# The rotary halves of the queries exchanged by on-chip transfers in place of TensorE products, in a decoder step on one core

## The reference

```python
def rope(x, pos):
    inv = ROPE_THETA ** (-jnp.arange(0, QK_ROPE_DIM, 2, dtype=jnp.float32) / QK_ROPE_DIM)
    ang = pos[:, None] * inv[None, :]
    ...
    cos, sin = jnp.cos(ang), jnp.sin(ang)
    x1, x2 = jnp.split(x.astype(jnp.float32), 2, axis=-1)
    return jnp.concatenate([x1 * cos - x2 * sin, x2 * cos + x1 * sin], axis=-1).astype(x.dtype)

def mla_query(hn, w_dq, q_norm, w_uq, w_uk, pos):
    B, L, _ = hn.shape
    cq = rmsnorm(hn @ w_dq, q_norm)
    q = (cq @ w_uq).reshape(B, L, N_HEADS, QK_NOPE_DIM + QK_ROPE_DIM)
    q_nope, q_rope = q[..., :QK_NOPE_DIM], q[..., QK_NOPE_DIM:]
    q_rope = rope(q_rope, pos)
    q_lat = jnp.einsum('blhd,chd->blhc', q_nope, w_uk)
    return q_lat, q_rope
```

## Time and profile before

| | us |
|---|---|
| median of 3 runs | 737.13 (736.79 to 737.34) |
| the profiled execution | 736.92 |
| its span in the trace | 735.2 |
| TensorE busy in the span | 725.5 |
| GpSimd, ScalarE, VectorE busy | 534.0, 408.1, 306.4 |

### The profile page before, as it was taken

One profiled execution on the slowest core, in us unless ns is written; L12 is line 12 of the kernel. 1 busy time (PEld: TensorE's weight loads), 2 busy tenths in 40 slices (PEclk: granted clock), 3 DMA queues, 4 the chain that ended last, 5 costly groups with the idle time before them and its releaser, 6 DMA issues.

```text
span 735.2 us, 16667 instructions
## 1 busy us (share of the span) xinstructions
PE 725.5 (99%) x6251; PEld 709.0 (96%) x6251; DVE 306.4 (42%) x771; ACT 408.1 (56%) x741; POOL 534.0 (73%) x252
## 2 busy tenths in 40 slices
PE   9999999999999999999999999999999999999995
PEld 9999999999999999999999888799999999999994
DVE  5446986233323222232488766752233323221002
ACT  7877555455444444555677566654554444445442
POOL 5995778869878888889867122159878878888991
PEclk9999999999999999999999999999999999999998
DMA  7864445556776755565565898326556555555641
GB/s 261 274 201 141 133 158 181 196 173 223 246 234 233 233 175 184 195 202 195 180 250 191 292 374 299 127 80 208 173 160 195 189 177 187 178 172 199 201 144 60
DMA packets 44554, 144.68 MB, mean 197 GB/s; under 512 B 5618, under 2 KB 5874, under 8 KB 44242
## 3 DMA queue, kind: packets, MB, share of 16 engines
q1 hardware_dynamic: 44210, 143.50, 58.3%
q0 software_dynamic: 144, 0.40, 0.1%
q10 hardware_dynamic: 144, 0.02, 0.0%
HBM read 142.42 MB, written 1.48 MB: 196 GB/s over the span
## 4 chain that ended last, share of the span: by engine, by line
PE 98%; DVE 1%; ACT 1%; issue 0%; DVEq 0%; POOL 0%; POOLq 0%
PE ps L1329 29%; PE ps L1330 29%; PE ps L1331 29%; PE ps L1730 1%; PE ps L1706 1%; PE ps L1391 1%; PE ps L1392 1%; PE ps L1399 1%; PE ps L1650 1%; PE ps L1459 1%; PE ps L1374 1%; PE ps L1368 0%; PE ps L1577 0%; PE ps L1710 0%; PE ps L1636 0%; PE ps L1355 0%
## 5 line engine op out<-in xcount | busy, mean ns | idle before, releaser
L408 POOL TENSOR_TENSOR wlo<-raw,whi 128x1024 fp32r<-128x1024 f32 x221 | 526.6, 2406 | 182.8 <-ACT whi L474 182.8
L1329 PE MATMUL ps<-xhi,whi 128*128 128x264 f32 x1000 | 286.9, 287 | 0.0
L1330 PE MATMUL ps<-xlo,whi 128*128 128x264 f32 x1000 | 283.3, 283 | 0.0
L1331 PE MATMUL ps<-xhi,wlo 128*128 128x264 f32 x1000 | 283.2, 283 | 0.0
L474 ACT ACTIVATE whi<-raw 128x1024 fp32r<-128x1024 f32 x221 | 232.7, 1054 | 50.1 <-PE ps L1331 48.4
L1330 PEld LDWEIGHTS ps<-xlo,whi 128*128 128x128 f32 x1000 | 188.5, 189 | 0.2
L1329 PEld LDWEIGHTS ps<-xhi,whi 128*128 128x128 f32 x1000 | 188.3, 188 | 0.3
L1331 PEld LDWEIGHTS ps<-xhi,wlo 128*128 128x128 f32 x1000 | 187.5, 188 | 0.0
L1329 PE MATMUL ps<-ahi,whi 128*128 128x264 f32 x352 | 100.0, 284 | 0.0
L1331 PE MATMUL ps<-ahi,wlo 128*128 128x264 f32 x352 | 99.9, 284 | 0.0
L1330 PE MATMUL ps<-alo,whi 128*128 128x264 f32 x352 | 99.9, 284 | 0.0
(11 more groups left out here) (259 smaller groups left out, 1146.5 us busy)
## 6 DMA issues: line engine op xcount, KB each, us to landing
raw<-w_stream SPq DMA_DIRECT2D x221, 512.0 KB, 3.3
pg<-pages SPq DMA_DIRECT2D x64, 288.0 KB, 4.3
pg<-w_ukT SPq DMA_DIRECT2D x1, 2048.0 KB, 9.4
pg<-w_uv SPq DMA_DIRECT2D x1, 2048.0 KB, 9.4
h<-xT SPq DMA_DIRECT2D x4, 264.0 KB, 4.5
y_out<-h SPq DMA_DIRECT2D x4, 264.0 KB, 2.7
raw<-w_stream SPq DMA_DIRECT2D x4, 256.0 KB, 5.0
wsraw<-wsT SPq DMA_DIRECT2D x1, 512.0 KB, 5.4
```

Source lines behind the costliest of these rows:

```text
L408: pool.tensor_tensor(wlo[:, c % RING, :], raw[:, c % RING, :], whi[:, c % RING, :].bitcast(F32), ALU.subtract).then_inc(lo_ready, 1)
L1329: pe.matmul(out, whi_, mhi, start=start, stop=False)
L1330: pe.matmul(out, whi_, mlo, start=False, stop=False)
L1331: return pe.matmul(out, wlo_, mhi, start=False, stop=stop)
```

## The change

Three things change.

1. The exchange is done by four transfers per pair, issued on SyncE: each moves one strip of 32 partitions x 264 numbers of the sines' product `tt` to the neighbouring strip of `sq`. TensorE's `query_swap` is gone. VectorE writes the cosines' product to the pair's PSUM bank itself, and the sum waits for all four transfers (`rope_swapped`).
2. With the swaps gone, TensorE, VectorE and ScalarE take the pairs one at a time. ScalarE writes a head's high part ahead of its sample columns, and copies the turned pair p - 1 right behind the first head of pair p, ahead of the slab splits. VectorE's sum of pair p - 1 stands behind the rope products of pair p and ahead of the low part of its first head. `latents` and cTlo move to other pairs.
3. The transfer of w_ukT goes in four quarters, one behind each of the first four exchanges; a load stands behind each exchange from the second on.

```diff
@@ SyncE
+            def exchange(p):
+
+                sp.wait_ge(rope_sin, p + 1)
+                for z in range(4):
+                    to, of = slice(32 * z, 32 * z + 32), slice(32 * (z ^ 1), 32 * (z ^ 1) + 32)
+                    sp.dma_start(sq[to, p % 2, :], tt[of, 1 + p % 2, :]).then_inc(rope_swapped[p % 2], 16)
+
             sp.wait_ge(slab_used, QA_S)
-            sp.dma_start(ukT, w_ukT).then_inc(uk_in, 16)
-            for c in range(QA_S + 2 * RING, PR_S + 6):
-                load(c)
+            for p in range(PAIRS):
+                exchange(p)
+                if p < 4:
+                    heads = slice(p * H // 4, (p + 1) * H // 4)
+                    sp.dma_start(ukT[:, heads, :], w_ukT[:, heads, :]).then_inc(uk_in, 16)
+                if p:
+                    load(QA_S + 2 * RING + p - 1)
...
@@ ScalarE, queries(p)
                     wait_query(act, x)
+                    act.activation(ohi[:, 2 * p + e, :], ps[:, 1 + e, 0:T], ACT.Copy).then_inc(qnhi_done, 1)
                     act.activation(qns[:, 2 * p + e, :], ps[:, 1 + e, NP_:T], ACT.Copy).then_inc(qns_done, 1)
-                    act.activation(ohi[:, 2 * p + e, :], ps[:, 1 + e, 0:T], ACT.Copy).then_inc(qnhi_done, 1)
+                    if p and not e:
+                        turned_queries(p - 1)
                     done = splits_up_to(min(QA_S + KQ * x // BLK + AHEAD + 1, PR_S + AHEAD), done)
...
@@ VectorE
                 wait_query(dve, 3 * p)
-                if p > 1:
-                    dve.wait_ge(rope_swap, p - 1)
-                    dve.wait_ge(qr_done, p - 1)
                 dve.tensor_tensor(tt[:, 1 + p % 2, :], ps[:, 0, 0:T], sinb, ALU.mult).then_inc(rope_sin, 1)
-                dve.tensor_tensor(sq[:, p % 2, :], ps[:, 0, 0:T], cosb, ALU.mult).then_inc(rope_cos, 1)
+                if p == 0:
+                    dve.wait_ge(psum_read, QA_N)
+                elif p == 1:
+                    dve.wait_ge(krlo_done, 1)
+                    kr_ready(dve)
+                else:
+                    dve.wait_ge(qrlo_done, 2 * p - 2)
+                dve.tensor_tensor(turned_bank(p), ps[:, 0, 0:T], cosb, ALU.mult).then_inc(rope_cos, 1)
...
                 dve.wait_ge(rope_cos, p + 1)
-                dve.wait_ge(rope_swap, p + 1)
+                dve.wait_ge(rope_swapped[p % 2], 64 * (p // 2 + 1))
...
+            for p in range(1, PAIRS):
+                query_rope(p)
+                query_turned(p - 1)
+                query_low(p, 0)
+                if p == 3:
                     latents(1)
-                if g == 2:
+                query_turned_low(p - 1)
+                if p == 5:
                     dve.memset(qsr[ROPE:P, 0], 0.0).then_inc(qsr_done, 1)
                     dve.memset(qsr[0:ROPE, 1], 0.0).then_inc(qsr_done, 1)
-                if g == 3:
+                if p == PAIRS - 1:
                     latents_low()
-                query_low(2 * g + 1, 1)
...
+                query_low(p, 1)
+                if p == 2:
+                    latents(0)
+            query_turned(PAIRS - 1)
...
@@ TensorE
-            queries(1)
-            for p in range(2, PAIRS, 2):
-                query_swap(p - 2)
-                query_swap(p - 1)
+            for p in range(1, PAIRS):
                 queries(p)
-                queries(p + 1)
-            query_swap(PAIRS - 2)
-            query_swap(PAIRS - 1)
...
-                pe.wait_ge(uk_in, 16)
+                pe.wait_ge(uk_in, 64)
```

More of the change, by code:

```diff
@@ L231, in build @@
         raw_ready = [sem(f"raw_ready{r}") for r in range(RING)]
+        rope_swapped = [sem(f"rope_swapped{r}") for r in range(2)]
         raw_first, raw_second, hi_first, lo_first = map(sem, ("raw_first", "raw_second", "hi_first", "lo_first"))
@@ L260, in build @@
             sem, ("gqs_done", "c_done", "ct_done", "cthi_done", "ctlo_done", "zero_done"))
[L262 to L263 removed]
+        q_done, qnhi_done, qlow_done, rope_cos, rope_sin, qr_done, qrhi_done, qrlo_done = map(
+            sem, ("q_done", "qnhi_done", "qlow_done", "rope_cos", "rope_sin", "qr_done", "qrhi_done", "qrlo_done"))
         qns_done, qrs_done, qsr_done, ql_done, qla_done, qlb_done, qlt_done, qsla_done, qslb_done = map(
@@ L377, in _ @@
                     numbers.append(page_number(2 + x // PAGES, x % PAGES))
-            sp.wait_ge(slab_used, QA_S)
-            sp.dma_start(ukT, w_ukT).then_inc(uk_in, 16)
-            for c in range(QA_S + 2 * RING, PR_S + 6):
-                load(c)
+            def exchange(p):
[3 more added lines that the diff above has]
+                    sp.dma_start(sq[to, p % 2, :], tt[of, 1 + p % 2, :]).then_inc(rope_swapped[p % 2], 16)
+            sp.wait_ge(slab_used, QA_S)
+            for p in range(PAIRS):
[5 more added lines that the diff above has]
+                    load(QA_S + 2 * RING + p - 1)
+            assert QA_S + 2 * RING + PAIRS - 1 == PR_S + 6
             sp.wait_ge(ql_done, 2)
@@ L1151, in _ @@
             keys_turned_low()
[L1152 to L1160, removed]
-                query_turned_low(2 * g - 1)
-                query_low(2 * g, 1)
-                if g == 1:
-                    latents(0)
-                query_rope(2 * g + 1)
-                query_low(2 * g + 1, 0)
-                if g == 1:
+            for p in range(1, PAIRS):
[3 more added lines that the diff above has]
+                if p == 3:
                     latents(1)
-                if g == 2:
+                query_turned_low(p - 1)
+                if p == 5:
                     dve.memset(qsr[ROPE:P, 0], 0.0).then_inc(qsr_done, 1)
                     dve.memset(qsr[0:ROPE, 1], 0.0).then_inc(qsr_done, 1)
-                if g == 3:
+                if p == PAIRS - 1:
                     latents_low()
-                query_low(2 * g + 1, 1)
-            for p in (PAIRS - 2, PAIRS - 1):
-                query_turned(p)
-            query_turned_low(PAIRS - 2)
+                query_low(p, 1)
+                if p == 2:
+                    latents(0)
+            query_turned(PAIRS - 1)
             def keys_low(p):
@@ L1565, in query_chunk @@
                         last.then_inc(q_done, 1)
-            def query_swap(p):
-                pe.wait_ge(rope_sin, p + 1)
-                if p == 0:
-                    pe.wait_ge(psum_read, QA_N)
-                elif p == 1:
-                    pe.wait_ge(krlo_done, 1)
-                    kr_ready(pe)
-                else:
-                    pe.wait_ge(qrlo_done, 2 * p - 2)
-                pe.matmul(turned_bank(p), swap, tt[:, 1 + p % 2, :], start=True, stop=True).then_inc(rope_swap, 1)
             def queries(p):
```

5 lines of the change are left out of this document (1 added, 4 removed).

## The result

| | before | after |
|---|---|---|
| median, us | 737.13 | 748.65 (748.24 to 751.75) |
| ratio to before, 95% interval | | 1.0166 (1.0155 to 1.0178) |
| the profiled execution | 736.92 | 751.75 |
| its span | 735.2 | 750.0 |

The kernel became slower by 11.5 us, where 5.9 were forecast. 748.65 lies 0.65 above the end of the range.

What follows compares the result with a forecast made beforehand. TensorE, busy 725.5 of 735.2 us, was taken as the bound. Stalls 2.6 + 1.3 + 2.3 + 1.1 + 2.1 = 9.4, less 3.56 for removed exchange products, gave 5.9 us more: 743.0 us, range 739.0 to 748.0.

Steps and rivals of the forecast that it cites:

- Slower: Whole kernel: a measured time above 738.6 us, chance 0.87.
- cTlo at the keys: End of the query stage: the keys' first product waits for VectorE's cTlo, behind pair 6's turned low parts, 2.1 us.
- the order alone with instant transfers: Query stage, landing under 0.5 us and closer issues: only step order left, +0.9 to +1.7; within the draw rival, 0.09.
- stall 1: TensorE ahead of pair 2's chunk 1: waits for the low part of pair 1's first head, 2.6 us.
- the price of one exchange: SyncE's four transfers per pair: 1.35 us to the fourth issue plus 2.5 landing, 3.85 us in all.
- the slower rival: Query stage: from a 3.0 us landing on, the exchange sets the pace; at 3.6, +9.9, 747 us; chance 0.14.
- The ring: Query stage: VectorE and ScalarE steps take 3.8 us against a pair's 3.26; pairs 3, 5, 6, 7 stall 2.3 us.
- pair 4: Query stage: load q8 waits for slab q4's split and delays exchange 2; TensorE stalls 1.1 us.
- Stall 2: TensorE ahead of pair 2's chunk 2: ScalarE's turned copies and slab split delay pair 1's second head, 1.3 us.
- The clock: TensorE behind two gaps over 2 us: half clock for 4 us costs 2 us each, 745 to 747; rival, chance 0.08.
- landing 3.6 and a little of the clock: Upper end of the range for the whole kernel: 3.6 us landing plus some lower-clock time, 748.0 us.

Runs made afterwards that it cites:

- experiment 1: The changed kernel without the 32 exchange transfers and VectorE's wait for them, the new order kept: 740.03 us, ratio 1.0039.
- experiment 2: The changed kernel with exchange 0 ahead of load q7, later loads one exchange later, w_ukT quarters behind exchanges 2 to 5: 745.62 us, ratio 1.0107.
- experiment 8: The kernel of before with w_ukT in four quarters between the loads, nothing else: 736.77 us, ratio 0.9999.
- experiment 4: The changed kernel with filler products on TensorE, 36 ahead of pair 2's chunk 1 and 18 ahead of the keys: 747.83 us, ratio 1.0144.
- experiment 9: The kernel of experiment 7 with w_ukT whole, issued by ScalarE beside exchanges 0 and 1: 743.82 us, ratio 1.0091.
- experiment 3: The changed kernel with the w_ukT quarters behind exchanges 4 to 7 instead of 0 to 3: 750.65 us, ratio 1.0181.
- experiment 7: The changed kernel with each pair's sum, copies and turned low parts moved later, cTlo one pair earlier, and SyncE's order of experiment 2: 739.77 us, ratio 1.0035.
- experiment 11: The kernel of experiment 7 with the w_ukT quarters issued by ScalarE, one in each of its pairs 2 to 5, ahead of the heads: 740.62 us, ratio 1.0038.
- experiment 12: The kernel of experiment 11 with the quarters at the end of ScalarE's pairs and loads q8 to q12 issued by ScalarE too: 740.25 us, ratio 1.0048.
- experiment 5: The changed kernel with VectorE's cTlo step moved from pair 7 to pair 6, ahead of the turned low parts: 747.60 us, ratio 1.0144.
- experiment 10: The kernel of experiment 9 with loads q8 to q12 also issued by ScalarE: 744.78 us, ratio 1.0106.

## Why the prediction was right or wrong

**Direction, and the chain: right.** Slower had 0.87. SyncE's first exchange issue behind load q7, VectorE's wait for it ahead of the low part, TensorE's gap in pair 2, the late load of q8 (387.95 where 384 to 386 was forecast), cTlo at the keys: each is in the trace, in the forecast's order. For the order alone with instant transfers the forecast had 738 to 738.7 and about 2 us at the keys; experiment 1 has 1.9 at the keys and 738.57 in its trace, but 740.03 in the median. Experiment 2 shows the main cause of stall 1, experiment 8 that the quarters cost nothing by themselves.

**The step that failed: the price of one exchange.** It was put at 3.85 us from the first issue to the last landing, 1.35 of it issues and 2.5 landing, and that one price was used for all eight. A quiet exchange did cost that: 3.7 to 3.9 us in the trace of after and in experiments 2, 4 and 9, though with other parts (1.9 issues at 0.63, 2.0 landing). But exchanges 0 to 4 took 5.7, 4.7, 3.9, 5.5 and 7.0 us in after, first issue to last landing. The longest, 3 and 4, have a quarter and a load, 1 MB, issued just ahead of them; exchange 2, behind a load alone, was as quick as forecast. The forecast named this ("transfers that queue behind a 512 KB load and a quarter of w_ukT") as the point at which the slower rival decides, with a chance of 0.14, and kept it out of the sum. The earlier trace rows gave a warning: a 512 KB load lands in 3.3 us and 2 MB in 9.4, so such transfers last long enough to be under way beside an exchange. What that costs was shown by experiments 3 and 9.

By terms: stall 1 was 2.15 us too small, of which exchange 0's own length is 1.9 (5.73 against 3.85). The ring and pair 4 were put at 3.35 and came to 6.5, the excess in pairs 5 and 6, which wait for VectorE behind exchanges 3 and 4 with their 5.5 and 7.0 us. Stall 2 was too large by 0.8: ScalarE had more time while VectorE stood. The keys' 2.1 was 2.42. The 0.95 behind waited products had no term. The forecast's terms as they stand add up to 5.8, not 5.9. That the cosines' product takes no longer into a PSUM bank was right (0.43), though the rows named for it all write SBUF.

**The clock: right mechanism, wrong chance.** The rival said that two gaps of over 2 us would each cost about 2 us; it had 0.08. It happened, 1.45 us for each in the trace, and 0.8 to 1.6 in all by the medians and ratios of experiment 4. The forecast itself had a stall of 2.6 directly followed by one of 1.3, and 2.1 at the keys, but put the clock at nothing in the sum. The Trainium skill's rule ("TensorE: Matmul & The Clock Gate", Part 1: the clock is at half after idling) was given as unseen for gaps this short; now the traces agree with it behind 4.6 us, and also show the lower clock behind 1.9 to 2.3 us, gaps shorter than those that the page gives.

**The range** ended at 748.0 with "landing 3.6 and a little of the clock", so 747 and 1 us for the clock. Slow landings (for part of the exchanges) and two falls of the clock happened at once; each was a rival with a chance of its own, and the end of the range held only a third of the 2.9 us that the two falls cost in the trace.

**What stays open.** The profiled execution took 3.1 us more than the median; which term varies between executions wasn't seen. It is not the time at the lower clock: the mean granted clock was 0.993 in the profiled execution and lower, 0.988 to 0.990, in the four shorter ones, so the 1.45 for each fall holds for that trace alone. Nor is it settled why exchange 0 took 5.7 us from its first issue in after (5.1 in experiment 3, without a quarter behind it) and 4.1 in experiment 2. After has two loads issued in the 3.1 us ahead of it, experiment 2 one; no run tests that.

## What to carry to other kernels

A small on-chip transfer has no fixed price: it depends on what is under way beside it, here some 2 us to land alone, 4 to 7 beside 1 to 2 MB, whichever engine issues them. Before one is put where an engine waits for it, list the bytes that are issued in the few us ahead of it, on all queues. And when cheap products are taken from the bounding engine, time first the new order with the replacement left out: here that one run (740.0 against 737.1) said that in this order there was nothing to win, however fast the replacement.

## What the runs showed of the hardware

- Issues of the 33 KB transfers on SyncE take 0.59 us each at the median (0.51 for the first of four, up to 1.3), against 0.33 to 0.43 for the loads and w_ukT in before. A load right behind an exchange also takes 0.58, in experiment 2 at 377.50.
- Landing of 33 KB from SBUF to SBUF on 32 partitions: 2.0 us at the least, 2.9 median, 4.7 at most in after, 1.8 to 1.9 in quiet exchanges (exchange 2 of experiments 2 and 9), medians of 5.8 and 7.2 beside 2 MB of another queue. The Trainium skill ("DMA: Bandwidth & Descriptors", anatomy of one DMA) has a fixed part of about 2.0, for transfers issued by GpSimd: the least rows of these, issued by SyncE, come near it.
- The granted clock was seen at 0.50 behind idle gaps of TensorE of 4.6 and 2.3 us (after), 2.0 (experiment 2), 2.2 (experiment 7) and 1.9 (experiments 11 and 12), and in the profiled executions not behind gaps of 1.8 (experiment 1) and 1.7 (experiment 4). In after it is 0.50 for 3.4 us each time (383.9 to 387.3, 414.6 to 418.1), in experiments 2, 3, 5, 9 and 10 for 6.8.
- The first product behind each wait costs 0.1 us more than the wait shows: its successor starts 0.22 behind it instead of 0.12.
